# A decoder layer on one core: joints between stages rejoined, and constant products on TensorE in three waits

## The reference

```python
x = x + 0.5 * swiglu1(rmsnorm(x))          # 1024 -> 2816 -> 1024
h = rmsnorm(x); z = h @ W_in               # [RWKV-7 | mLSTM | two gates]
x = x + (sigmoid(gA) * (rwkv7(z) @ W_upA) + sigmoid(gB) * (mlstm(z) @ W_upB)) @ W_out
x = x + cross_attention(rmsnorm(x), rmsnorm(mem))   # 4 heads, 256 memory tokens
x = x + 0.5 * swiglu2(rmsnorm(x))
out = rmsnorm(x)
```

## Time and profile before

| | |
|---|---|
| median of 3 runs | 2820.5 us (2817.25 to 2822.07) |
| profiled execution: time | 2816.52 us |
| profiled execution: span from first to last instruction | 2814.7 us |
| TensorE busy | 2730.4 us (97%), 14234 matmuls |
| DVE, ACT, POOL busy | 1364.8, 805.1, 1513.6 us (48%, 29%, 54%) |
| mean granted TensorE clock | 0.99 of full speed |

### The profile page before, as it was taken

One profiled execution on the slowest core, in us unless ns is written; L12 is line 12 of the kernel. 1 busy time (PEld: TensorE's weight loads), 2 busy tenths in 40 slices (PEclk: granted clock), 3 DMA queues, 4 the chain that ended last, 5 costly groups with the idle time before them and its releaser, 6 DMA issues.

```text
span 2814.7 us, 35894 instructions
## 1 busy us (share of the span) xinstructions
PE 2730.4 (97%) x14234; PEld 2263.7 (80%) x14234; DVE 1364.8 (48%) x1379; ACT 805.1 (29%) x1205; POOL 1513.6 (54%) x903
## 2 busy tenths in 40 slices
PE   6999999999999998999999989999999999999998
PEld 5788888888788877887888778889987888888886
DVE  8443432023656635777777745453447444441103
ACT  4333332112000112444444322123313333331111
POOL 4988884223894623555555534330135988882221
PEclk9999999999999999999999999999999999999998
DMA  2323227361664655335244254212021323329151
GB/s 110 132 106 119 90 105 312 137 231 60 232 234 172 224 211 159 100 104 167 86 116 109 83 208 149 76 60 112 31 90 65 124 111 120 117 97 361 62 191 71
DMA packets 144521, 383.14 MB, mean 136 GB/s; under 512 B 10477, under 2 KB 61933, under 8 KB 130177
## 3 DMA queue, kind: packets, MB, share of 16 engines
q1 hardware_dynamic: 110144, 299.92, 30.4%
q10 hardware_dynamic: 34240, 81.30, 7.8%
HBM read 272.57 MB, written 108.58 MB: 135 GB/s over the span
## 4 chain that ended last, share of the span: by engine, by line
PE 78%; issue 10%; POOL 7%; DVE 3%; DMA 1%; ACT 1%; SPq 1%; ACTq 0%; POOLq 0%; DVEq 0%
PE G L1077 15%; PE G L1078 15%; PE G L1079 15%; PE G L1002 8%; PE G L1004 8%; PE G L1003 8%; PE G L1247 2%; POOL AL L886 2%; PE G L1546 1%; PE G L1528 1%; PE G L1284 1%; DVE nt_b L2196 1%; POOL Tr L882 1%; DMA nmb<-rows_d 0%; POOL rho L868 0%
## 5 line engine op out<-in xcount | busy, mean ns | idle before, releaser
L959 POOL TENSOR_TENSOR whi<-raw,zero 128x1024 fp32r<-128x1024 f32 x67 | 140.1, 2091 | 431.7 <-PE G L1004 344.5
L1077 PE MATMUL G<-hhi,v_hi 128*128 128x512 f32 x800 | 312.0, 390 | 0.0
L1079 PE MATMUL G<-hhi,v_lo 128*128 128x512 f32 x800 | 311.2, 389 | 0.0
L1078 PE MATMUL G<-hlo,v_hi 128*128 128x512 f32 x800 | 311.2, 389 | 0.0
L943 POOL TENSOR_TENSOR v_lo<-sum_temp,v_hi 128x512 fp32r<-128x512 f32 x88 | 115.0, 1307 | 357.3 <-ACT v_hi L1759 357.3
L1002 PE MATMUL G<-hhi,whi 128*128 128x512 f32 x688 | 271.0, 394 | 22.6 <-POOL wlo L962 20.2
L1003 PE MATMUL G<-hlo,whi 128*128 128x512 f32 x688 | 269.4, 392 | 0.0
L1004 PE MATMUL G<-hhi,wlo 128*128 128x512 f32 x688 | 269.4, 392 | 0.0
L1247 PE MATMUL G<-hq,gw 128*128 128x512 f32 x768 | 219.6, 418 | 17.4 <-DVE ev L2557 14.7
L1077 PE MATMUL G<-t_hi,whi 128*128 128x512 f32 x480 | 186.9, 389 | 0.0
L1079 PE MATMUL G<-t_hi,wlo 128*128 128x512 f32 x480 | 186.7, 389 | 0.0
(11 more groups left out here) (426 smaller groups left out, 6264.8 us busy)
## 6 DMA issues: line engine op xcount, KB each, us to landing
a_d<-act_new SPq DMA_DIRECT2D x20, 2048.0 KB, 6.3
atile<-a_d SPq DMA_DIRECT2D x36, 1024.0 KB, 9.9
gw<-gw_d SPq DMA_DIRECT2D x32, 1024.0 KB, 5.3
raw<-in_wg SPq DMA_DIRECT2D x44, 512.0 KB, 4.1
sum_temp<-in_wd ACTq DMA_DIRECT2D x82, 256.0 KB, 3.5
xT<-in_wu SPq DMA_DIRECT2D x40, 512.0 KB, 4.5
gw_d<-gw SPq DMA_DIRECT2D x16, 1024.0 KB, 4.7
hhi<-a_d SPq DMA_DIRECT2D x18, 512.0 KB, 15.8
```

What stands on the lines that cost most here:

```text
L959: nc.gpsimd.tensor_tensor(whi[:, k, 0:w], raw[:, k, 0:w], zero[:].to_broadcast([P, w]), ALU.add).then_inc(hi_made, 1)
L1077: nc.tensor.matmul(dst, wh, hi, start=start, stop=False, skip_group_check=True)
L1078: nc.tensor.matmul(dst, wh, lo, start=False, stop=False, skip_group_check=True)
L1079: return nc.tensor.matmul(dst, wl, hi, start=False, stop=stop, skip_group_check=True)
```

## The change

- *Kernel start.* SP issues the vectors, the first weight unit and the first x chunk; ACT the second unit. POOL splits the first 256 columns of both units (`FIRST`) before the other 768. ACT loads its exponential table at once. DVE's squares are added two chunks late. TensorE multiplies a matrix of ones by itself (`spare`), 8 times when the first unit has landed and 4 times when the first x chunk has.
- *Start of both FFNs.* ACT makes the up units' hi part, which POOL made. The norm's sum is 8 products of one column (token on the partition), the root is made on 128x8, spread by one product with a diagonal (`zd`); ACT copies the gate products out of their banks (`gs`) before the root exists. POOL's block sums wait for the sum (`h_pe sum`) in place of `gs`. In `ffn(1)` TensorE does seven chunks of the first unit, seven of the second, then the last chunk of both. Token sums stand in two pairs, before and after the root.
- *Mixers.* Fills 0 to 4 and 29 to 31 alternate between two banks and wait one emptying less. DVE's additions to the mLSTM memory (`CN`) move from the end of a segment behind step `ssc` of the next. At level 4 product Mv stands ahead of the fill. `decays(0)` is issued behind the store of fill 1; three memsets move behind fill 2.
- *Merge.* `y_d` chunks are loaded and split in pieces, two before the last segment's store.
- *Final norm.* The last of four squares is not added by DVE: TensorE sums it in a second group of four products. The root's own half is spread first. In the last half 3 and 5 spare products stand behind the two groups.

```diff
+            if not f:
+                pe.wait_ge(ones_made, 1)
+                pe.wait_ge(raw_in[0], 16)
+                spare(8, G[3][:, 1, 0:P], ones[:])
+                pe.wait_ge(xc_in[0], 16)
+                spare(4, G[3][:, 1, 0:P], ones[:])
+            if f:
+                for r in range(2):
+                    unit_ready(c.unit + r)
+                    for t in range(KD - 1):
+                        if r == 0:
+                            norm_chunk(t)
+                        gate_tile(r, t)
+                norm_chunk(KD - 1)
+                for r in range(2):
+                    gate_tile(r, KD - 1)
...
-            norm(nt, T)
...
+            pe.wait_ge(*f_lo.at(f, 1))
+            up(0, 0)
...
+            for n in range(KD):
+                last = nc.tensor.matmul(G[nb][:, 1, n:n + 1], nt[:, n * P:(n + 1) * P], con(C_ONES, 1), start=True,
+                                        stop=True)
+            last.then_inc(*h_pe.sig("sum"))
+            up(0, 1).then_inc(f_prod.sem, 1)
...
+            for h in range(NHALF):
+                last = nc.tensor.matmul(G[0][:, h, :], con(C_ONES), zd[:, h * HALF:(h + 1) * HALF], start=True, stop=True)
+            last.then_inc(*h_pe.sig("sp"))
+            pe.wait_ge(*f_lo.at(f, 2))
+            up(1, 0)
+            up(1, 1).then_inc(f_prod.sem, 1)
...
-                take(hi, raw[:, r, :])
-                pool.wait_ge(*f_lo.at(f, 2 * r + 1))
+                pool.wait_ge(*h_act.at(f"v{r}", f - 1))
                 tt(lo, raw[:, r, :], hi.bitcast(F32), ALU.subtract).then_inc(f_lo.sem, 1)
...
                 if q == 0:
-                    pool.wait_ge(*f_gs.at(f, 1))
+                    pool.wait_ge(*h_pe.at("sum", f - 1))
...
+                    both = 0 < f < FILL_AT[0] or f > FILL_AT[NSEG]
+                    pe.wait_ge(ev_made, f if both else f + 1)
...
-                last = nc.tensor.matmul(G[3][:, 1, :], gw[:, k, way == 2, t * P:(t + 1) * P],
+                last = nc.tensor.matmul(bank_fill(f), gw[:, k, way == 2, t * P:(t + 1) * P],
...
             for r in range(2):
                 dve.wait_ge(*h_act.at(f"c{r}", f - 1))
+                tt(gs[:, r, :], gs[:, r, :], flat(G[0][:]), ALU.mult).then_inc(f_gs.sem, 1)
...
+            act.wait_ge(*f_gs.at(f, 2))
+            activation(nrx[:], flat(G[0][:]), ACT.Copy).then_inc(*h_act.sig("nrx"))
```

More of the change, by code:

```diff
@@ new lines, in ffn, with up @@
+            nb = 2 + c.dve % 2
+            def up(r, h):
+                bank, cols = G[nb] if r else G[5 - nb], slice(h * HALF, (h + 1) * HALF)
+                for t in range(KD):
+                    s, w = 2 * r + t // RC, slice(t % RC * P, (t % RC + 1) * P)
+                    last = three(bank[:, h, :], v_hi[:, s, w], v_lo[:, s, w], hhi[:, t, cols], hlo[:, t, cols],
+                                 t == 0, t == KD - 1)
+                return last
+            pe.wait_ge(*f_lo.at(f, 1))
@@ L1781, in ffn @@
[L1781 to L1787 removed]
+                up_hi(f)
+                act.wait_ge(store, 2 * KD * 16)
+            own = f"ffn{f + 1}_norm"
+            for k in range(RC):
+                act.wait_ge(*nh_dve.at(f"l{k % 2}", c.norm - 4 + k // 2))
+                activation(xT[:, k, right], xT[:, k, right], ACT.Copy, scale=v1(own, k)).then_inc(*h_act.sig(f"x{k}"))
```

379 lines of the change are left out of this document (244 added, 135 removed).

## The result

The changed kernel takes 2806.0 us, the median of 7 executions (2798.98 to 2811.22), against 2820.5 for 7 of the kernel before: a ratio of 0.9946 (95% interval 0.9933 to 0.9958), 14.5 us faster. The forecast was 2782, with 2770 to 2793 as its widest range. The direction was right; the gain is less than half of the 37 us that I summed. The changed kernel also varies more, over 12 us where the kernel before varies over 9, and its profiled execution is one of the long ones: 2811.15 us, with a span of 2809.3 against 2814.7. So the two traces differ by 5.4 us only.

What follows compares the result with a forecast made beforehand. TensorE was busy 97% of the span, so only its idle and half-speed time could be won. Six terms summed to 37.2 us, taking 2816.5 to 2779.3; 2.7 added for the median gave 2782, widest range 2770 to 2793.

Steps and rivals of the forecast that it cites:

- First FFN: Kernel start to block 0: first product at 10.5 at full clock, block 0 at 61.1; 14.2 us won, ends 8 and 17.
- the clock isn't kept: Rival, chance 0.13: spare products don't hold TensorE's clock; 2.7 us lost at the start, 1.6 at the end; 2787.
- Second FFN: Its start: the 4.50 us wait and 2.7 of half speed go, the new sum costs 1.9; 5.2 us won.
- Start of the mixers: Fills 1 to 4 no longer wait for emptied banks, fill 5 starts 9.8 us earlier; 10.2 us won, ends 6 and 11.
- I leave 0.5 for a `gw` that lands late: Start of the mixers: allowance of 0.5 us for a fill's weights landing late, taken off 10.7 us.
- Joints: Between segments: waits for alpha and the level 4 fill go, but `myo` slips; 0.5 us won, ends -4 and +10.5.
- The bound: At the joints: product A can't come earlier than `myo` + 16.9 us, because of the decays' loads.
- The slip: At the joints: `myo` comes later as DVE's `dec` and scan run beside POOL; 0.35 to 1.35 us, taken as 0.9.
- so each joint gives 0.9 - 0.9: At each joint: 0.9 us won is cancelled by 0.9 of slip; only the first and last segments' fill waits remain, 0.5 us.
- my rival on the slower side: Chance 0.03: DVE's run from `dec` to `kmod` keeps POOL from `myo`; eight joints pay 5.5 us each, 2827.
- End of the mixers: Last fills and merge: merge starts 1.3 us earlier, two of its later waits shrink by 2.1; 3.4 us won, ends 1 and 5.5.
- Final norm: Middle loses 0.8 us, the root's half comes 4.4 earlier if spare products keep the clock; 3.7 us won, ends 1.5 and 4.5.

Runs made afterwards that it cites:

- best_no_spares: best with all spare products taken out, at the start and in the final norm; 2771.2 us, 0.9824 of the kernel before.
- best: copies_first plus c_loads_first's early merge loads, with segment 0's decays issued behind fill 5's weights; 2771.3 us, 0.9829 of the kernel before.
- c_loads_first: copies_first with all four loads of the merge's first half issued ahead of the last store, not two; 2781.5 us, 0.9869 of the kernel before.
- copies_first: Changed kernel with ScalarE's copies (`vtok` among them) ahead of the two exponentials that need the decays' loads; 2784.1 us, 0.9877 of the kernel before.
- c_decays_later: copies_first with segment 0's decays' loads issued one fill later, behind fill 4's weights; 2782.8 us, 0.9876 of the kernel before.
- b_first: Changed kernel with only VectorE's mask of B put ahead of `qe`; 2795.8 us, 0.9917 of the kernel before.

## Why the prediction was wrong

Two steps failed that carry 25 of the 32 us by which the traces fall short of the sum (37.2 summed, 5.4 found); smaller misses are the rest. By the prediction's own terms:

- *First FFN, 14.2 forecast, 13.3 found.* The first product was at 11.80, not 10.5, at full clock as forecast; the ups began at 34.72 (forecast 34.5) and block 0 at 62.09 (61.1), the spread having waited 1.73 for `zd` where I had put 1.5 for all waits. The working of the inside was wrong in one point, which the sum doesn't use. I valued the full clock of the first products at 2.7 us, and the rival "the clock isn't kept" charged it; best_no_spares shows it is worth nothing, for VectorE sets the pace of this stretch.
- *Second FFN, 5.2 and 4.9.* Right, by its own steps.
- *Start of the mixers, 10.2 and 1.3.* The step "I leave 0.5 for a `gw` that lands late" failed. It was 5.6 us of wait, and behind it a fill of 7.8 us, at half clock up to 1061, where 5.5 is full speed. The kernel before had a sign of it that I misread: I wrote that fills 1 to 4 waited for an emptying, but its fill 3 (at 1067.55) waited 1.29 us for `gw`. I counted what SP is freed from and not what its queues then carry together: the decays' loads on their way for 15 us, and the next weights behind them 12. Besides, the low-rank products waited 2.06 for `lora`, which the waits at the fills had covered. best has the forecast mechanism without the decays in the way: fill 5 starts 33.9 us behind the gate row's product (forecast 34.6), and the 10.5 us that it wins up to A are my 10.2.
- *Joints, 0.5 and -15.8.* The bound was right: A can't come before the end of `myo` + 16.9. In the slow joint above `myo` ends at 1478.13, which gives 1495.0, and A is at 1495.09; over the seven joints the distance is 16.96 to 17.41 (16.81 to 17.26 in the kernel before). The slip was about right as well: `myo` ends 3.40 us behind VectorE's `hm` there and 2.63 in the joint of the earlier trace rows, 0.8 later for my 0.9. The step that failed is the next: "so each joint gives 0.9 - 0.9". I took a bound that stays as a time that stays. But TensorE now stood idle for 2 us at that bound, where before it came to it 0.1 us early, and I had charged 2.7 us for just such an idle stretch in three other places. By that rule each of the seven waits could have lost up to 2.7, 19 us in all, and the forecast would have reached 2801; A and Mu's product lose 1.5 of it where the clock falls. That `qe` then meets GpSimd (2.2 more) I could have read from the kernel before: in its segment 0 the two do meet, with `qe` at 2.85 us, and in segments 1 to 6 `qe` is ahead by 0.5 at most. Of my rival on the slower side the mechanism was the wrong one (VectorE's run from `dec`), its place, the joint, the right one.
- *End of the mixers, 3.4 and 0.3.* I had looked at where `wlo` stands against the fills' end, 1651.94, and taken it as fixed. Two DMA issues moved in ahead of ScalarE's report hold up the request for the weights; the first product came 1.8 us later against the fills and not 1.3 earlier, which is the 3.1 missing, and c_loads_first gives 2.3 of it. The merge's two later waits (1.12 and 1.67) are gone entirely, 0.7 more than forecast, but the products behind the wait of 5.62 run at a granted clock of 0.55 until 1659.5, which I had not charged.
- *Final norm, 3.7 and 1.4.* The sum's start was won (2.4 us) and most of it lost again: the spread starts only 0.6 earlier against the last product, behind the last square and the spare products, where I had 0.7 + 0.9, and its clock wasn't kept. The rival "the clock isn't kept" had this half right.

The Trainium skill (TensorE: Matmul & The Clock Gate, Part 1) has the moment at which the clock changes vary from run to run. The traces here agree: of the seven waits of 1.99 to 2.44 us for `vtok` in one execution, two were followed by an A at full speed (1.16), four by one of 1.84 to 2.08, and in one the clock fell within A (1.40, then 1.92 for Mu's product). It would explain the spread of the changed kernel's times, 12 us over seven executions against 5 over four of copies_first; that the other executions differ by their number of slow segments is only argued, since one was traced, and the kernel before varies over 9 us without such waits.

By the Trainium skill (SBUF — State Buffer, Who interferes with whom) a VectorE operation with two inputs in SBUF contends with a GpSimd operation that reads SBUF: whichever starts first keeps the other out for its whole length. I asked of it only what the scan does to `myo`. `myo` takes 1.94 us in six of the seven joints (2.09 in the first) and took 1.28 in the earlier trace rows, which agrees; the whole slip, 0.8, is less than the 1.35 that I had drawn from the rule. What I didn't think through is that the same holds later in the segment, with VectorE as the one that waits: `qe` has two such inputs, and its end 2.93 us behind GpSimd's start agrees as well.

## What to carry to other kernels

A wait that a change removes ahead of a bound that stays doesn't just give nothing: the engine arrives early, idles at the bound, and what idling costs there (the clock, the order in which two engines meet) comes on top; price the wait at the bound by the same rule as all others. When loads are moved into a quiet place, look for the next load that someone waits for, and put the moved ones behind the last of these. And a stretch that another engine paces gets nothing from a faster clock, so test a device such as spare products by leaving it out.

## What the runs showed of the hardware

- In the changed kernel VectorE's `qe`, 512 elements wide, took 0.69 us where it started 0.06 or 0.07 us ahead of GpSimd's multiplication, and 2.85 to 2.90 where it started 0.04 to 0.08 behind it (three segments). In all fourteen traces, wherever it started 0.04 to 2.2 us behind the start of a GpSimd operation of 128x1024 that takes 2.4 us (`AL` or `Tr`), it ended 2.91 to 2.95 us behind that start; where it started 2.3 us or more behind, it took 0.69.
- Three loads that spread a row over 128 partitions, 256 KB each, hold back a load of 1 MB asked for 4 to 6 us later: it took 12 us in the changed kernel and 13 in copies_first and c_decays_later, where 5.4 is the median.
- Eight spare products of 128 columns in a wait of 2 us kept the full clock in seven segments of seven, where without them it fell in five of seven (two of seven in b_first). Five such products in the last norm's wait left the spread slower than full speed in eleven traces of twelve.
- Segment 3, whose later slots hold no fills, took 69.2 to 72.8 us in the seven kernels with the copies first and the additions moved, whose segments 1, 2, 4, 5 and 6 agree within 0.3. What decides it wasn't tried.
